# Opening of a fused two-block network reordered, and the idle products of TensorE taken out

## The chip, the cores and the metric

The kernel runs on one core of a Trainium2 chip. The metric is the device time of one execution in microseconds; smaller is better. The engines are named as in the profile: PE is TensorE (PEld its weight loads), DVE is VectorE, ACT is ScalarE, SP is SyncE, which issues all the DMAs here. hi and lo are the two parts into which an fp32 value is split for products in the fast format fp32r; a full product is hi x hi + lo x hi + hi x lo.

## The reference, cut

Two networks one after the other, on 256 tokens of width 1024, each two layers deep.

```python
# first block, layer l; x: tokens, xc: context tokens (256 each)
shift_x, scale_x, gate_x = split(silu(c) @ w_mod[l] + b_mod[l], 3)         # the same for c_ctx
hx = rmsnorm(x, norm_w[l]) * (1 + scale_x) + shift_x                        # the same for hc
px = hx @ w_in[l]          # retention, short conv, conformer conv, attention, gates
merged = sum(sigmoid(gate_i) * (branch_i @ w_branch[l, i]) for i in range(4))
x = x + gate_x * (merged @ w_out[l])
# second block, layer i; mod = silu(c_2) @ ada_w[i] + ada_b[i], six parts
h = rmsnorm(x, g0) * (1 + sc_m) + sh_m
y = rglru_mixer(h) if i == 0 else gla_mixer(h)
x = x + gt_m * rmsnorm(y, g1)
h = rmsnorm(x, g2) * (1 + sc_f) + sh_f
x = x + gt_f * rmsnorm(conv_ffn(h), g3)
```

## The kernel before, in words

Activations lie transposed: 8 tiles of 128 channels by 256 tokens (512 with the context, in layer 0 of the first block). Weights stream from HBM through a ring of three slabs of 1 MB (`stream`, SP's loop at line 1166). Each slab holds two weight tiles, the units; ACT writes the high part of a unit (line 1236), DVE the low part (line 1944), into four slots. `project` (line 610) makes one output tile: 8 products hi x hi, 8 with the low tokens, 8 with the low weights (lines 625, 627, 630). `project_group` (line 634) starts three tiles together and takes the token tiles in turn as they become ready (lines 601 to 603). Each result goes to one of 8 PSUM banks in turn and is evacuated by ACT (line 1222) or DVE.

The order of work is written by hand on each engine, with counting semaphores between them; a wait holds all that stands behind it on its engine.

The opening: SP issues params, the first table columns, the rows of c and c_ctx (1 MB, already spread over all partitions), then pairs of modulation weights (`start_pair`: a scale block of 1 MB for DVE, a shift block of 1 MB for PE), x, ctx, and the first weight slabs. ACT makes silu of the rows (line 1332). DVE makes the scales: each block of 128 outputs is a multiply and reduce over 1024 against a row (line 1977). PE makes the shifts (`shift_rows`, line 660: silu(c) as stationary operand; `shift_cols`, line 668: turned into columns). ACT squares x (line 1279), PE sums the squares over channels (`sum_all`, line 676), ACT takes the root, DVE the reciprocal (line 1845). DVE then writes normed tiles (line 1855), ACT their high parts with the shift (line 1316), DVE the low parts (line 1864), and the first group of projections starts. Behind it DVE computes the decays (lines 2020 to 2048) and, between other work, reductions for the second block's modulation (line 1981), whose weights SP issues between slabs (`IN_MODS`). The 31-tap convolution (line 2226) is DVE's longest piece; the weighted keys (line 2250) that PE needs at line 786 stand behind it.

`keep_clock(n)` (line 570) writes n products of a table with itself into the next free bank. Nobody reads them. It stands ahead of places where PE would wait: in the first merge, ahead of the output projections of each layer, in the RG-LRU and GLA outputs, in the sums ahead of GLA, and three times in `ffn`. The call in the retention loop never runs, since step 1 has a projection there in both layers. In `ffn` and ahead of GLA the stop is: sums of y (line 1001), residual on DVE, squares on ACT (line 1625), `sum_pairs` on PE (line 684, 16 passes), root, reciprocal, normed pairs, then the next projections.

Of the kernel before, what the change touches and what calls it, by code (L numbers as in the profile page):

```python
# [25 lines left out]
P = 128  # L26
# [28 lines left out]
IN_STAGE, IN_MODS = "in", (4, 4, 4, 3, 3, 3, 3)  # L55
# [55 lines left out]
def program(nc, io, counts):  # L111

    ctx = ExitStack()
    with ctx:
# [29 lines left out]
        c_rows_landed, c2_landed, shapes_landed = sem("c_rows_landed"), sem("c2_landed"), sem("shapes_landed")  # L144
# [164 lines left out]
        lam8, lam8n = small[:, 240:248], small[:, 248:256]  # L309
        warm = sbuf("warm", 16)  # L310
# [238 lines left out]
        def _(pe):  # L549
# [153 lines left out]
            for l in range(2):  # L703
# [113 lines left out]
                for n, (hd, g) in enumerate(units):  # L817
                    ret_scores(hd, g)
                    if n in in_ret:
                        project(in_ret[n], nx)  # L820
                    elif n == 1:
                        keep_clock(8)
                    if n:
                        ret_out(*units[n - 1])
# [95 lines left out]
                keep_clock(3 if l == 0 else 5)  # L920
# [44 lines left out]
            def ffn(l):  # L965
                keep_clock(9)
# [4 lines left out]
                keep_clock(3 if l else 7)  # L971
# [5 lines left out]
                keep_clock(7)  # L977
# [65 lines left out]
            keep_clock(4)  # L1043
# [4 lines left out]
            keep_clock(9)  # L1048
            sum_pairs("n2 1")
            keep_clock(7)  # L1050
# [72 lines left out]
            keep_clock(7)  # L1123
# [5 lines left out]
        def _(sp):  # L1129
            sp.dma_start(params[:], io["params"]).then_inc(params_landed, 16)  # L1130
            sp.dma_start(tables[:, 0:EARLY], io["tables"][:, 0:EARLY]).then_inc(early_landed, 16)
            sp.dma_start(shapes, io["c_rows"][:, 0:2 * D]).then_inc(c_rows_landed, 16)

            def start_pair(i):

                w = io["w_mod_t"][0][D + 256 * i:D + 256 * i + 256, :].rearrange("(j p) k -> p j k", p=P)
                sp.dma_start(start_blocks(START + i), w).then_inc(start_landed[START + i], 16)
                sp.dma_start(start_slot(i), by_rows(io["w_mod"][0])[:, :, 256 * i:256 * i + 256])\
                    .then_inc(start_landed[i], 16)
# [22 lines left out]
            start_pair(0)  # L1162
            sp.dma_start(xT[:, :, 0:S], by_rows(io["x"])).then_inc(x_landed, 16)
            sp.dma_start(xT[:, :, S:2 * S], by_rows(io["ctx"])).then_inc(x_landed, 16)
            start_pair(1)
            for n, (name, src, _) in enumerate(stream):
                if name == "w rgo 0":

                    sp.wait_ge(*vector.did(f"expo 1.{HEADS - 1}"))
                    sp.wait_ge(*scalar.did(f"q_dec 1.{HEADS - 1}"))  # L1170
                    sp.dma_start(level, io["level"]).then_inc(late_landed, 16)
                    sp.dma_start(gla_a, io["gla_w_alpha_2"][0]).then_inc(late_landed, 16)
                if n == 2:
# [25 lines left out]
                if RING + 1 <= n <= RING + len(IN_MODS):  # L1199
                    due.append((n, IN_STAGE, n - RING - 1, None))  # L1200
# [13 lines left out]
        def _(act):  # L1214
# [105 lines left out]
            def start_shift(k):  # L1320

                if k in (4, 6):
# [5 lines left out]
            def silu_rows(n):  # L1328

                act.wait_ge(c_rows_landed, 16 * n)  # L1330
# [6 lines left out]
            silu_rows(1)  # L1337

            for l in range(2):
                nx = 2 * S if l == 0 else S  # L1340
                groups = (0, 1) if l == 0 else (0,)
                if l == 0:
# [11 lines left out]
                act.wait_ge(shapes_landed, 16 * (l + 1))  # L1354
                if l == 0:

                    act.wait_ge(tables_landed, 16)
                    act.wait_ge(c2_landed, 16)
                    nc.scalar.activation(c2_row, c2_row, ACT.Silu).then_inc(*scalar.does("c2 row"))
                    at = PARAM_AT["decay"][0]  # L1360
                    nc.scalar.activation(lp[0], params[:, at:at + 24], ACT.Abs).then_inc(*scalar.does("lp abs"))
                    act.wait_ge(*scalar.did("lp abs"))
                    nc.scalar.activation(lp[1], lp[0], ACT.Exp, scale=-1.0).then_inc(*scalar.does("lp exp"))
# [462 lines left out]
        def _(dve):  # L1826
# [162 lines left out]

            def start_blocks_done(i):  # L1990

                dve.wait_ge(start_landed[i], 16)
                for j in range(2):
                    modulate_block("mod", 0, 2 * i + j, start_blocks(i)[:, j, :], start_scratch)
                vector.now[f"start mod {i}"] = vector.n
# [56 lines left out]
            for l in range(2):  # L2052
# [4 lines left out]
                if l == 0:  # L2057
                    dve.wait_ge(early_landed, 16)
                    dve.wait_ge(*scalar.did("c rows 1"))
# [6 lines left out]
                    for k in (0, 2, 4, 6):  # L2066
                        if k > 2:
                            start_blocks_done(START + k // 2)
                            low(k - 2)
                            low(k - 1)  # L2070
# [4 lines left out]
                        if k == 2:  # L2075
                            split_to(3)
                            low(0)
                            low(1)
# [4 lines left out]
                dve.wait_ge(shapes_landed, 16 * (l + 1))  # L2083
                dve.wait_ge(tables_landed, 16)
# [61 lines left out]
                if l == 0:  # L2146
                    settled()
                    for n in range(BT):
                        short_in(n, False)
                        if n == 0:  # L2150
                            decays()
                            dve.wait_ge(*scalar.did("c2 row"))
                        else:
                            mod_blocks(mod_plan[IN_STAGE, n - 1])
                    for k in range(SC_K):
# [740 lines left out]
```

## Time and profile before

| | us |
|---|---|
| runs, lowest / median / highest of 3 | 1831.96 / 1834.66 / 1835.02 |
| profiled execution | 1834.24 |
| its span, first to last instruction | 1832.5 |
| PE busy | 1765.7 (96%) |
| PE weight loads busy | 1564.7 (85%) |
| DVE busy | 1438.4 (78%) |
| ACT busy | 894.4 (49%) |
| mean granted clock of PE, of full | 0.994 |

The ends of matmuls are modelled, so a busy PE is not PE at its peak. An fp32 product runs as two passes, each an instruction of its own. On the timeline the bracket gives the idle time of the engine before the instruction and what ended it.

### The profile page before, as it was taken

How to read it: one execution, taken by the hardware profiler on the slowest of the kernel's cores; microseconds unless marked ns; L12 is line 12 of the kernel's file. 1: busy time of each engine (PE TensorE's matmuls, PEld its weight loads, DVE VectorE, ACT ScalarE, POOL GpSimd, SP SyncE). 2: the span in 40 equal slices, each digit the busy share in tenths (PEclk: the TensorE clock that was granted, in tenths of full speed). 3: DMA queues.
4: the chain of work that ended last, by engine and by line, in shares of the span. 5: the costliest groups of instructions: out<-in, count | busy, mean ns of one | idle time of the engine just before them, and what ended most of it. 6: DMA issues, size and time to landing. Idle time of an engine off the chain costs nothing.

```text
span 1832.5 us, 29617 instructions
## 1 busy us (share of the span) xinstructions
PE 1765.7 (96%) x11364; PEld 1564.7 (85%) x11364; DVE 1438.4 (78%) x2491; ACT 894.4 (49%) x1528; POOL 0.2 (0%) x4
## 2 busy tenths in 40 slices
PE   4999999999999999999999999999999989999998
PEld 1788887777888887988978999988999979989998
DVE  5789995558899898797866799878887478869864
ACT  3322334456232334443355755676656466567553
POOL 0000000000000000000000000000000000000000
PEclk8999999999999999999999999999999999999999
DMA  9564321212777776553421599552555625226543
GB/s 346 199 237 145 115 70 44 73 37 74 257 242 244 262 254 227 167 155 106 136 93 58 176 330 310 162 174 92 185 186 171 196 69 162 92 93 207 185 157 120
DMA packets 242332, 302.77 MB, mean 165 GB/s; under 512 B 6016, under 2 KB 223360, under 8 KB 241680
## 3 DMA queue, kind: packets, MB, share of 16 engines
q1 hardware_dynamic: 242192, 300.87, 49.9%
q8 instruction: 92, 1.51, 0.4%
q14 instruction: 48, 0.39, 0.1%
HBM read 299.79 MB, written 1.05 MB: 164 GB/s over the span
## 4 chain that ended last, share of the span: by engine, by line
PE 43%; DVE 8%; ACT 4%; issue 3%; DMA 0%; DVEq 0%; ACTq 0%
PE bank L625 10%; PE bank L627 10%; PE bank L630 10%; PE bank L601 2%; PE bank L603 2%; PE bank L602 2%; ACT w_hi L1236 1%; DVE w_lo L1944 1%; PE bank L956 1%; PE bank L957 1%; PE bank L958 1%; DVE stats L1845 1%; PE bank L684 1%; PE bank L1032 0%; DVE arena L2645 0%
## 5 line engine op out<-in xcount | busy, mean ns | idle before, releaser
L1944 DVE TENSOR_TENSOR w_lo<-ring,w_hi 128x1024 fp32r<-128x1024 f32 (+2 forms) x444 | 500.3, 1135 | 199.9 <-ACT w_hi L1236 197.3
L1236 ACT ACTIVATE w_hi<-ring 128x1024 fp32r<-128x1024 f32 (+2 forms) x444 | 434.2, 985 | 170.9 <-PE bank L630 95.9
L625 PE MATMUL bank<-h_hi,w_hi 128*128 128x256 f32 (+2 forms) x2366 | 418.2, 319 | 0.4
L630 PE MATMUL bank<-h_hi,w_lo 128*128 128x256 f32 (+2 forms) x2366 | 410.4, 315 | 0.0
L627 PE MATMUL bank<-h_lo,w_hi 128*128 128x256 f32 (+2 forms) x2366 | 410.4, 315 | 0.0
L625 PEld LDWEIGHTS bank<-h_hi,w_hi 128*128 128x128 f32 x2366 | 344.9, 188 | 35.5 <-issue 2.6
L627 PEld LDWEIGHTS bank<-h_lo,w_hi 128*128 128x128 f32 x2366 | 346.0, 188 | 29.9
L630 PEld LDWEIGHTS bank<-h_hi,w_lo 128*128 128x128 f32 x2366 | 346.1, 188 | 29.8
L1222 ACT ACTIVATE work<-bank 128x512 f32<-128x512 f32 (+1 forms) x138 | 68.3, 509 | 262.0 <-PE bank L630 194.5
L1222 ACT ACTIVATE arena<-bank 128x256 f32<-128x256 f32 (+4 forms) x125 | 56.5, 453 | 218.2 <-PE bank L630 148.3
L2226 DVE SCALAR_TENSOR_TENSOR arena<-arena,params 128x512 f32<-128x512 f32 (+1 forms) x240 | 131.1, 631 | 0.0
L1981 DVE CUSTOM_DVE_ANT_0 arena<-arena,c_row,params 128x1024 f32<-128x1024 f32 x96 | 120.1, 1281 | 11.6 <-DMA arena<-in_ada_w_t 11.5
L601 PE MATMUL bank<-h_hi,w_hi 128*128 128x256 f32 (+2 forms) x306 | 94.1, 308 | 18.2 <-DVE h_lo L1864 9.1
L1222 ACT ACTIVATE work<-bank,params 128x256 f32<-128x256 f32 x88 | 49.6, 564 | 90.4 <-DVE w_lo L1944 57.0
L602 PE MATMUL bank<-h_lo,w_hi 128*128 128x256 f32 (+2 forms) x306 | 91.8, 300 | 0.0
L603 PE MATMUL bank<-h_hi,w_lo 128*128 128x256 f32 (+2 forms) x306 | 91.7, 300 | 0.0
L601 PEld LDWEIGHTS bank<-h_hi,w_hi 128*128 128x128 f32 x306 | 59.3, 194 | 24.4 <-issue 12.5
L1977 DVE CUSTOM_DVE_ANT_0 arena<-arena,tables,params 128x1024 f32<-128x1024 f32 x48 | 60.7, 1282 | 18.8 <-DMA arena<-in_w_mod_t 18.8
L2588 DVE SCALAR_TENSOR_TENSOR work<-bank,params,work 128x255 f32<-128x255 f32 x88 | 42.4, 482 | 32.3 <-ACT work L1222 32.2
L625 PE MATMUL bank<-arena_r,w_hi 128*128 128x512 f32 (+2 forms) x306 | 64.8, 338 | 1.9 <-ACT w_hi L1236 1.7
L627 PE MATMUL bank<-arena_r,w_hi 128*128 128x512 f32 (+2 forms) x306 | 64.6, 337 | 0.0
L630 PE MATMUL bank<-arena_r,w_lo 128*128 128x512 f32 (+2 forms) x306 | 64.5, 337 | 0.0
(296 smaller groups left out, 2227.6 us busy)
## 6 DMA issues: line engine op xcount, KB each, us to landing
ring<-in_w_in SPq DMA_DIRECT2D x86, 1024.0 KB, 5.7
arena<-in_ada_w_t SPq DMA_DIRECT2D x96, 512.0 KB, 6.1
ring<-in_ffn_w_up SPq DMA_DIRECT2D x44, 1024.0 KB, 5.1
ring<-in_w_branch SPq DMA_DIRECT2D x32, 512.0 KB, 4.9
arena<-in_w_mod_t SPq DMA_DIRECT2D x32, 512.0 KB, 5.4
ring<-in_ffn_w_down SPq DMA_DIRECT2D x16, 1024.0 KB, 5.1
ring<-in_gla_w_in SPq DMA_DIRECT2D x12, 1024.0 KB, 5.4
ring<-in_w_out SPq DMA_DIRECT2D x8, 1024.0 KB, 6.3
```

The source lines that it names most:

```text
L601: pe.matmul(out, ws[0][:, k, :], hi, start=start, stop=False)
L602: pe.matmul(out, ws[0][:, k, :], lo, start=False, stop=False)
L603: return pe.matmul(out, ws[1][:, k, :], hi, start=False, stop=stop)
L625: pe.matmul(out[:, 0:n], w[0][:, k, :], hi(k, n), start=k == 0, stop=False)
L627: pe.matmul(out[:, 0:n], w[0][:, k, :], lo(k, n), start=False, stop=False)
L630: m = pe.matmul(out[:, 0:n], w[1][:, k, :], hi(k, n), start=False, stop=k == tiles - 1)
L1222: return nc.scalar.activation(dst, src, func, **kw)\
L1236: nc.scalar.activation(w_hi[u % PARTS][:, 0:src.shape[1], :], src, ACT.Copy)\
L1944: step(nc.vector.tensor_tensor(w_lo[u % PARTS][:, 0:nk, :], src, w_hi[u % PARTS][:, 0:nk, :].bitcast(F32), ALU.subtract), f"lo {u}", *(["u ...
L1977: step(nc.vector.tensor_tensor_reduce(w if v else scratch, w, c_rows[:, v, :], 1.0, param("b_mod", 2)[:, l, c:c + 1], ALU.mult, ALU.add, m ...
L1981: step(nc.vector.tensor_tensor_reduce(w, w, c2_row, 1.0, param("ada_b", 2)[:, l, c:c + 1], ALU.mult, ALU.add, mod2[l][:, c:c + 1]), name)
L2226: step(nc.vector.scalar_tensor_tensor(dst, src, cw[:, l, k, n:n + 1], dst, ALU.mult, ALU.add), name)
```

## The change

- c rows: the two loads of rows (c and c_ctx, c_2) go. DVE makes six tiles `c_diag` (each four 128x128 pieces: the identity times a column of silu(c)), PE multiplies them by ones (6 products of 128x512), ACT copies the results into `c_rows` and `c2_row`.
- Order of loads: both first scale blocks, x, ctx, the first shift block, slab 0, the second shift block, slab 1, then the other four blocks, slab 2, tables. `IN_AT` issues later reductions' weights up to one slab earlier.
- PE: the sums of squares first, then shift rows 0 and 1. ACT and DVE: weight splits in smaller steps between the normed tiles; the decays move to the time in which DVE waits for the rows.
- All calls of `keep_clock` go, and the function.

```diff
-IN_STAGE, IN_MODS = "in", (4, 4, 4, 3, 3, 3, 3)
+IN_STAGE, IN_MODS, IN_AT = "in", (4, 4, 4, 3, 3, 3, 3), (4, 5, 6, 7, 7, 8, 9)
+        c_diag = [t[:] for t in dve_t] + [stat, stat2]
-            def keep_clock(n):
-                b = state_["bank"]
-                if b >= BANKS:
-                    pe.wait_ge(*emptied(order[b - BANKS]))
-                for _ in range(n):
-                    pe.matmul(psum[b % BANKS][:, 0:S], ones, tables[:, 0:S], start=True, stop=True)
 # PE, opening
                     pe.wait_ge(early_landed, 16)
+                    for i in range(6):
+                        out = open_bank(f"c row {i}")
+                        pe.wait_ge(*vector.did(f"c diag {i}"))
+                        pe.matmul(out[:], ones_pp, c_diag[i], start=True, stop=True)\
+                            .then_inc(*tensor.does(f"filled c row {i}"))
+                    sum_all("n1 0", 2 * S, KT)
                     shift_rows(0)
-                    sum_all("n1 0", 2 * S, KT)
                     shift_cols(0)
 # PE, the idle products (places: 8 in the retention loop, never run; then as they run)
-                        if l == 0 and b == MERGE_ORDER[0] and i == 0:
-                            keep_clock(6)
-                keep_clock(3 if l == 0 else 5)        # ahead of out {l}
-                keep_clock(9)                         # ffn: ahead of the sums
-                keep_clock(3 if l else 7)             # ffn: ahead of the projections
-                keep_clock(7)                         # ffn: ahead of the down projection
-            keep_clock(4)                             # ahead of the RG-LRU output
-            keep_clock(9)                             # n2 1: ahead of the sums
-            keep_clock(7)                             # n2 1: behind the sums
-            keep_clock(7)                             # ahead of the GLA output
 # SP
-            sp.dma_start(shapes, io["c_rows"][:, 0:2 * D]).then_inc(c_rows_landed, 16)
-            start_pair(0)
+            start_scales(0)
+            start_scales(1)
             sp.dma_start(xT[:, :, 0:S], by_rows(io["x"])).then_inc(x_landed, 16)
             sp.dma_start(xT[:, :, S:2 * S], by_rows(io["ctx"])).then_inc(x_landed, 16)
-            start_pair(1)
+            start_shifts(0)
+                if n == 1:
+                    start_shifts(1)
                 if n == 2:
-                    start_pair(2)
-                    start_pair(3)
+                    for i in (2, 3):
+                        start_scales(i)
+                        start_shifts(i)
+                if n == 3:
                     sp.dma_start(tables[:, EARLY:shapes_at], ...).then_inc(tables_landed, 16)
-                    sp.dma_start(c2_row, io["c_rows"][:, 2 * D:3 * D]).then_inc(c2_landed, 16)
+                due += [(n, IN_STAGE, i, None) for i, at in enumerate(IN_AT) if at == n]
 # ACT
-            silu_rows(1)
+            (abs and exp of the decays, moved here)
+            for i in range(6):
+                row = c2_row if i >= 4 else c_rows[:, i // 2, :]
+                evacuate(f"c row {i}", row[:, 512 * (i % 2):512 * (i % 2) + 512], ...)
-                    square_all("n1 0", 2 * S, KT, lambda k: xT[:, k, :], also=lambda k: k == 3 and shift_row(0))
+                    square_all("n1 0", 2 * S, KT, lambda k: xT[:, k, :])
                     deviation("n1 0", 2 * S, D)
+                    split_to(1)
+                    shift_row(0)
                     shift_col(0)
+                    split_to(2)
                     shift_row(1)
-                    split_to(1)
                     shift_col(1)
-                    split_to(3)
                     modulated("n1 0", ..., start_shift, both_hi)      # start_shift(3) now does split_to(3)
 # DVE
+                    for i in range(6):
+                        for j in range(4):
+                            ins = nc.vector.tensor_scalar(c_diag[i][:, P * j:P * j + P], ident,
+                                                          csil[:, 4 * (i % 2) + j, i // 2:i // 2 + 1], None, ALU.mult)
+                    decays()
                     dve.wait_ge(*scalar.did("c rows 1"))
                     start_blocks_done(START)
                     start_blocks_done(START + 1)
                     inverse("n1 0", 2 * S)
-                    for k in (0, 2, 4, 6): ...
+                    modulation1(0, 0, 4); split_to(1); tile(0); tile(1); split_to(2); low(0); low(1)
+                    tile(2); tile(3); split_to(3); low(2); low(3)
+                    start_blocks_done(START + 2); ...; tile(4); tile(5)
+                    start_block_done(START + 3, 0); low(4); low(5); start_block_done(START + 3, 1)
+                    ...; tile(6); tile(7); low(6); low(7)
```

## Rows read from the trace of the kernel before

**Rows 1.** The page, part 2: TensorE's granted clock in tenths, 40 slices of 45.8 us.
```profile
PEclk8999999999999999999999999999999999999999
```

**Rows 2.** The instructions of line 576: duration in ns, first and last start.
```profile
L576 PE MATMUL bank<-tables x166: 377/379/382, 446.3 to 1763.0; 128*128 128x256 f32 x166
```

**Rows 3.** Stretches: length, PE PEld DVE ACT POOL busy, PEclk, DMA share, GB/s.
```profile
40.00:45.00 5.00, 2.63 (x6) 2.15 (x7) 5.00 (x9) 0.44 (x2) 0.00 (x0) 0.50 1.08 367
...
811.40:814.70 3.30, 3.30 (x9) 2.59 (x8) 3.30 (x7) 0.00 (x0) 0.00 (x0) 0.50 0.13 42
...
1596.00:1600.00 4.00, 4.00 (x24) 4.00 (x23) 1.85 (x6) 0.97 (x2) 0.00 (x0) 0.57 0.94 313
```

**Rows 4.** Timeline of the opening: start, length in us, instruction, idle before.
```profile
9.47 2.00 ACT L1332 ACTIVATE tables<-tables 128x1024 f32<-128x1024 f32 x2 [5.01 <-DMA tables<-in_c_rows]
...
12.25 1.28 DVE L1977 CUSTOM_DVE_ANT_0 arena<-arena,tables,params 128x1024 f32<-128x1024 f32 x1 [12.25 <-DMA arena<-in_w_mod_t]
...
21.19 2.19 ACT L1279 ACTIVATE work<-xT 128x512 f32<-128x512 f32 x4 [9.71 <-DMA xT<-in_ctx]
...
21.87 7.13 PE L676 MATMUL bank<-work,tables 128*128 128x512 f32 x16 [0.96 <-ACT work L1279]
...
29.86 3.35 DVE L1845 RECIPROCAL stats<-stats 128x512 f32<-128x512 f32 x1 [1.25 <-ACT stats L1222]
...
42.37 0.77 PE L601 MATMUL bank<-h_hi,w_hi 128*128 128x512 f32 x1 [8.87 <-DVE h_lo L1864]
...
48.72 3.62 PE L660 MATMUL bank<-arena,small 128*2 128x256 f32 x16
...
64.57 1.68 DVE L1864 SCALAR_TENSOR_TENSOR h_lo<-work,mods,h_hi 128x256 fp32r<-128x256 f32 x4 [4.84 <-ACT h_hi L1316]
...
69.80 1.98 PE L625 MATMUL bank<-h_hi,w_hi 128*128 128x512 f32 x8
```

**Rows 5.** Timeline, behind the opening: DVE at 142 us, PE at 256 us.
```profile
141.88 1.28 DVE L1981 CUSTOM_DVE_ANT_0 arena<-arena,c_row,params 128x1024 f32<-128x1024 f32 x1 [3.83 <-DMA arena<-in_ada_w_t]
...
255.89 3.90 PE L786 MATMUL bank<-arena 128*128 128x128 f32 x32 [1.03 <-DVE arena L2250]
```

**Rows 6.** Timeline of PE: the norm stop of ffn 0; the sums ahead of GLA.
```profile
1262.14 4.05 PE L576 MATMUL bank<-tables 128*128 128x256 f32 x18
...
1268.31 5.38 PE L684 MATMUL bank<-work,tables 128*128 128x256 f32 x16 [2.12 <-ACT work L1625]
...
1273.52 3.19 PE L576 MATMUL bank<-tables 128*128 128x256 f32 x14
...
1278.11 0.36 PE L601 MATMUL bank<-h_hi,w_hi 128*128 128x256 f32 x1 [1.41 <-DVE h_lo L1911]
...
1475.41 4.31 PE L684 MATMUL bank<-work,tables 128*128 128x256 f32 x16 [1.25 <-ACT work L1625]
```

**Rows 7.** Timeline of PE, ACT and DVE at idle products followed by ready work.
```profile
448.28 2.00 ACT L1332 ACTIVATE tables<-tables 128x1024 f32<-128x1024 f32 x2
...
1139.59 2.32 PE L576 MATMUL bank<-tables 128*128 128x256 f32 x10
...
1144.95 0.35 PE L601 MATMUL bank<-h_hi,w_hi 128*128 128x256 f32 x1 [1.26 <-ACT h_hi L1556]
...
1403.09 3.18 PE L576 MATMUL bank<-tables 128*128 128x256 f32 x14
...
1411.33 2.96 DVE L1944 TENSOR_TENSOR w_lo<-ring,w_hi 128x1024 fp32r<-128x1024 f32 x3 [0.16 <-ACT w_hi L1236]
...
1760.23 3.18 PE L576 MATMUL bank<-tables 128*128 128x256 f32 x14
...
1770.05 0.36 PE L956 MATMUL bank<-w_hi,h_hi 128*128 128x256 f32 x1 [0.96 <-ACT w_hi L1236]
```

**Rows 8.** Who PE waited for: us in total, times, longest.
```profile
PE bank L601 <- ACT arena L1222: 2.0, 1, 2.0
...
PE bank L625 <- ACT w_hi L1236: 1.7, 1, 1.7
```

More of the change, by code:

```diff
@@ L143, in program @@
         start_landed = [sem(f"start_landed{i}") for i in range(2 * START)]
[L144 removed]
+        c_rows_landed, shapes_landed = sem("c_rows_landed"), sem("shapes_landed")
         x_landed, late_landed, out_landed = sem("x_landed"), sem("late_landed"), sem("out_landed")
@@ L1320, in start_shift @@
             def start_shift(k):
+                if k == 3:
+                    split_to(3)
                 if k in (4, 6):
@@ L1328, in silu_rows @@
             def silu_rows(n):
-                act.wait_ge(c_rows_landed, 16 * n)
+                act.wait_ge(c_rows_landed, 16 * (n - 1))
                 for v in range(2):
@@ L1336, in _ @@
             nc.scalar.activation(small[:, 32:56], param("c_vec"), ACT.Silu).then_inc(*scalar.does("csil"))
-            silu_rows(1)
+            at = PARAM_AT["decay"][0]
+            nc.scalar.activation(lp[0], params[:, at:at + 24], ACT.Abs).then_inc(*scalar.does("lp abs"))
+            act.wait_ge(*scalar.did("lp abs"))
+            nc.scalar.activation(lp[1], lp[0], ACT.Exp, scale=-1.0).then_inc(*scalar.does("lp exp"))
+            for i in range(6):
+                row = c2_row if i >= 4 else c_rows[:, i // 2, :]
+                evacuate(f"c row {i}", row[:, 512 * (i % 2):512 * (i % 2) + 512],
+                         also=["c rows 1"] if i == 3 else ["c2 row"] if i == 5 else [])
             for l in range(2):
@@ L1345, in _ @@
                     act.wait_ge(x_landed, 32)
-                    square_all("n1 0", 2 * S, KT, lambda k: xT[:, k, :], also=lambda k: k == 3 and shift_row(0))
+                    square_all("n1 0", 2 * S, KT, lambda k: xT[:, k, :])
                     deviation("n1 0", 2 * S, D)
+                    split_to(1)
+                    shift_row(0)
                     shift_col(0)
+                    split_to(2)
                     shift_row(1)
-                    split_to(1)
                     shift_col(1)
-                    split_to(3)
                     modulated("n1 0", (0, 1), lambda k, g: mod1[0][:, k, g:g + 1], start_shift, both_hi)
[L1354 to L1363, printed above, removed]
+                if l:
+                    act.wait_ge(shapes_landed, 32)
                 def first_out(kind, n, late):
@@ L1988, in mod_blocks, with start_block_done @@
                     modulate_block(*m, mod_slot(m), stats)
+            def start_block_done(i, j):
+                if j == 0:
+                    dve.wait_ge(start_landed[i], 16)
+                modulate_block("mod", 0, 2 * i + j, start_blocks(i)[:, j, :], start_scratch)
+                if j:
+                    vector.now[f"start mod {i}"] = vector.n
             def start_blocks_done(i):
[L1992 to L1995, printed above, removed]
+                start_block_done(i, 0)
+                start_block_done(i, 1)
             def modulation1(l, a, b):
@@ L2058, in _ @@
                     dve.wait_ge(early_landed, 16)
+                    dve.wait_ge(*scalar.did("csil"))
+                    for i in range(6):
+                        for j in range(4):
+                            ins = nc.vector.tensor_scalar(c_diag[i][:, P * j:P * j + P], ident,
+                                                          csil[:, 4 * (i % 2) + j, i // 2:i // 2 + 1], None, ALU.mult)
+                            step(ins, *([f"c diag {i}"] if j == 3 else []))
+                    decays()
                     dve.wait_ge(*scalar.did("c rows 1"))
@@ L2065, in _ @@
                                       both_hi, both_lo)
[L2066 to L2070, printed above, removed]
+                    after(f"start mod {START + 1}")
+                    modulation1(0, 0, 4)
+                    split_to(1)
+                    tile(0)
+                    tile(1)
+                    split_to(2)
+                    low(0)
+                    low(1)
+                    tile(2)
+                    tile(3)
+                    split_to(3)
+                    low(2)
+                    low(3)
+                    for k in (4, 6):
+                        if k == 4:
+                            start_blocks_done(START + 2)
+                        else:
+                            start_block_done(START + 3, 0)
+                            low(4)
+                            low(5)
+                            start_block_done(START + 3, 1)
                         after(f"start mod {START + k // 2}")
@@ L2074, in _ @@
                         tile(k + 1)
[L2075 to L2078, printed above, removed]
                     low(KT - 2)
@@ L2082, in _ @@
                 step(nc.vector.memset(cx[l][:, :, 0:ng, S + 1:S + 2], 0.0), f"cx z1 {l}")
-                dve.wait_ge(shapes_landed, 16 * (l + 1))
-                dve.wait_ge(tables_landed, 16)
+                if l:
+                    dve.wait_ge(shapes_landed, 32)
                 def grouped(ap):
@@ L2147, in _ @@
                     settled()
+                    dve.wait_ge(*scalar.did("c2 row"))
                     for n in range(BT):
                         short_in(n, False)
[L2150 to L2153, printed above, removed]
+                        if n:
                             mod_blocks(mod_plan[IN_STAGE, n - 1])
+                    dve.wait_ge(shapes_landed, 16)
+                    dve.wait_ge(tables_landed, 16)
                     for k in range(SC_K):
```

7 lines of the change are left out of this document (2 added, 5 removed).

## Prediction, made before the changed kernel ran

> **What bounds the kernel now.** I read the slices of the page first: after the opening, TensorE (PE) is busy in nearly every slice and its granted clock is full nearly everywhere [rows 1]. So the end is set by PE's own products, and a change pays only where it removes idle time of PE, products of PE, or time at half clock. Next the group of line 576: 166 instructions, 83 fp32 products of two passes each, which compute nothing [rows 2]. They stand at thirteen places. A pass starts every 0.216 us (18 of them last 4.05 us, the last one 0.38), so they hold PE for 36 us. What matters is not that sum but, place by place, whether PE would have waited anyway.
>
> Then the clock. Beyond the opening it falls three times, each time for some 3.4 us: a stretch at 0.50 after the wait at 809 to 811 us, one inside the sums at 1268, one after 1595 [rows 3]. What came before each: a PE wait of 2.0 us, of 2.1 us, and one much like them before 1595; the next shorter wait, 1.7 us, was followed by no fall [rows 6, 8]. I take from this that a wait of about 2 us can bring the fall and one below 1.7 us doesn't. The price: PE at 0.50 delivers half, so 3.3 us of pure products lose 1.65 us. In the sums of line 684, which wait for ScalarE (ACT) as well, it is less: 5.38 us with a fall against 4.31 us without, 1.07 us [rows 6].
>
> Last the opening, read engine by engine on the timeline [rows 4].
>
> **Part 1, the front.** Before: the rows of c land at 9.4 us, the first scale block at 12.1, x and ctx at 21.2, the sums run 21.87 to 29.0, the reciprocal ends at 33.2, the first projection starts at 42.37 at half clock, the grouped start ends at 69.80 [rows 3, 4].
> The change removes the load of the rows (1 MB) ahead of everything, and moves one shift load (1 MB) behind ctx. One such load took 2.6 us (9.45 to 12.1) and ctx lands after five of them, so x and ctx land near 18.1: 3.1 us earlier. Instead of the load, VectorE (DVE) makes 24 diagonal pieces of 128x128 and PE 6 products of 128x512, ACT 6 evacuations. None of these shapes stands in the opening. For PE the bounds are 0.43 us a pass (the sums at full clock, 7.13 us for 16) and twice that cold: 12 passes, 5.2 to 10.3 us from about 5.4 us on, so done between 10.6 and 15.7; I take 13. ACT and DVE work beside it. The two scale blocks (8 reductions of at most 1.28 us) then take DVE from about 14 to 24, still ahead of the reciprocal. So this stretch is hidden in the wait for x. If the products took 10 us more, DVE would become late at the reciprocal; that is the cover.
> The new risk: PE stands from 13 to 18.7, so the sums start at half clock. At full clock they take 7.1 us, wholly cold 13.7; part cold I take 1.6 us more. Sums end near 27.5 instead of 29.0, the reciprocal near 31.7 instead of 33.2.
> From there the order is new: DVE splits two weight tiles (about 1.15 us each, as in [rows 7]) ahead of the first normed tiles and one ahead of the first low part, where it split four; but both shift rows (3.6 us of PE each) now stand behind the sums, 27.5 to 36, and ACT's first high part behind them, near 37.6. The first low part ends at 38.4: the first projection starts 3.9 us earlier, and warm. After it DVE is the chain: two tiles' low parts, a split, low parts, four reductions (4.9 us), two tiles, two reductions, low parts, two reductions, tiles, low parts. Adding up, low part 6 is there at 60.8 and 7 at 61.7, against 65.4 for tile 6 before, and the group ends near 65.0: **4.8 us earlier**. Bounds: PE alone (8 tiles of 9 products at 0.23 us, two shift rows) could end at 62.4, -7.4; with sums wholly cold and one more fall, 67, -3.
> Behind the front, the chain of some thirty short DVE instructions for the decays leaves the stretch of the first projections, and the ada loads are issued earlier in the stream. Before, DVE waited 3.8 us for such a load at 141.88, went into the 31-tap convolution late, and made PE wait 1.03 us at 255.89 [rows 5]. With DVE's work gone and loads earlier this wait goes: **-1.0** (bounds 0 and -1.03). Front: **-5.8**, between -3 and -8.4.
>
> **Part 2, no idle products, work that PE did too early or too late.** At three places the next real product was ready behind the last idle one, so removal can move it. At 1403.09 (14 passes, 2.84 us) the down projection of block 0 can start at once; the fourth weight tile's low part, which DVE finishes at 1412.4 whatever PE does, then ends a wait of about 0.7 us: **-2.1** (bounds 0 and -2.84) [rows 7]. At 446.28 (12 passes, 2.4 us) the second branch tile's weights are split only behind ACT's 2.0 us of silu at 448.28, which gives most of it back: **-0.7** (bounds 0 and -2.4). At 1760.23 (14 passes) the same start gains nothing: PE waits at 1770.05 for a weight part that stands behind DVE's low parts, and the wait grows from 0.96 to 3.8 us [rows 7]. At 700.85 (6 passes, 1.1 us) and 1139.59 (10 passes) too the projection begins earlier and stops at the last merged tile, at the same time as before; the wait at 1144.95 grows from 1.26 to 3.2 us [rows 7].
>
> **Part 3, the clock.** The waits of PE that remain, products and wait together: 6.1, 4.5, 5.2, 4.5, 5.2, 2.8 us around the three norm stops of the FFNs and GLA (for instance 1262.14 to 1268.31 and 1273.52 to 1278.11) [rows 6], 5.0 us ahead of the GLA output, 3.8, 3.2, 2.8 and 1.9 us at the others. By the 2 us reading nearly all of them bring a fall; three falls are there before. Terms, each a price of a fall times how much of the stretch is real work of PE:
> - 1144.95: 1.65 x 0.75 = 1.2; 700.85 (1.9 us, at the border): 0.4; the output of RG-LRU at 1234 (2.8 us), where DVE's scan paces PE: 0.3.
> - norm stop of ffn 0: the sums already fell (1.07 in hand), now they start cold, and the projections behind 1278.11 start cold too: 1.7.
> - norm stop ahead of GLA: sums 1.0, less what the four spaced GLA products hide: 0.6.
> - norm stop of ffn 1: sums 1.0, projections 1.5: 2.5.
> - down projection of ffn 1: 1.5.
> - the falls at 811 and 1596 of this profile stay likely, not certain: -1.0.
> Sum **+7.2**; bounds 0 (no more falls than now) and twice the sums and starts, some +14.
> The Trainium skill, "TensorE: Matmul & The Clock Gate", section "Why this matters for your kernels", speaks against this change: long idle gaps between bursts put the clock back to half. By that sentence alone the longer waits all pay, as in my terms; the row at 811 shows that a wait of 2.0 us was enough here.
>
> **The sum** goes against the profiled execution: 1834.24 us, of which 1832.5 are span and 1.7 lie around it; it is 0.4 below the median of the runs (1834.66). 1834.2 - 5.8 - 2.1 - 0.7 + 7.2 = 1832.8; I forecast **1833.0**.
>
> **The rivals.**
> 1. The forecast, the two halves cancel: 1830.5 to 1836. For it: each term has a row. Chance 0.50.
> 2. Slower: the clock stays low through a whole norm stop. Mechanism: a wait of 4.5 to 6 us on either side of 16 sum passes, so the sums run cold from end to end (16 x 0.43 = 6.9 instead of 4.3 us, three times: +4.7 beyond the terms) and the two groups of projections behind them start with a second cold stretch (+1.6 each): 1833 + 8 = 1841. It decides if the sums, cold from their first pass, don't bring the clock back; against it, at 1268 the sums themselves brought it back before their end. Chance 0.14.
> 3. Faster: most waits of 2.6 to 3.8 us bring no fall, or one that other waits cover. Terms fall from 7.2 to about 3: 1829. For it, three falls are a small sample. Chance 0.15.
> 4. Faster, the front gives more: PE-bound from the first product, -7.4 and -1.0: 1830.4. Chance 0.11.
> 5. The front does less than it says: PE cold in the sums and the shift rows behind them, so that the first projection starts at 41: only -2: 1836.8. Chance 0.10.
>
> **The numbers.** Range 1828.5 to 1839.5: it takes in cases 1, 3, 4, 5 and part of case 2. 0.2% (3.7 us) is about what a measurement of this kernel can tell from no change, so faster means under 1831.0 and slower over 1838.3. Faster 0.27 (cases 3 and 4 and a little of 1), slower 0.16 (2 and a little of 5), same 0.57.
>
> **What would show it.** Right: no product of line 576; x squares at 18 us; sums ending 27 to 28; first projection 38 to 39; steady projections from about 65; no wait ahead of line 786; the down projection of ffn 0 straight behind its last projection; clock at 0.50 in eight to twelve stretches, and the sums of line 684 above 5 us in all three stops. Wrong: sums of line 684 at 4.3 us after waits of 5 us (case 3), or near 7 us (case 2); a grouped start ending after 67 (case 5).

## The result, and the profile after

| | before | after |
|---|---|---|
| median (lowest to highest), us | 1833.93 (1830.94 to 1835.02) | 1840.6 (1837.78 to 1842.96) |
| ratio of after to before, 95% | | 1.0036 [1.0027, 1.0045] |
| profiled execution / its span | 1834.24 / 1832.5 | 1842.96 / 1841.1 |
| PE busy / mean granted clock | 1765.7 / 0.994 | 1754.8 / 0.979 |

The change made the kernel 6.7 us slower, where I had forecast 1.7 us faster; the time lies above my range. The profiled execution of after is the slowest of its eight, 2.4 us above the median, that of before 0.3 above; so the traces show a loss of 8.6 us in the span, and I book that one and come back to the difference.

The page, part 2, granted clock in 40 slices, now with three eights behind 1240 us, where [rows 1] has only nines:

```profile
PEclk8999999999999999999999999998999989989999
```

Stretches of after, PE alone: length, PE busy and instructions, PEclk, DMA share, GB/s. They answer to [rows 3].

```profile
702.90:706.20 3.30, 3.30 (x9) 0.50 0.73 245
808.70:812.00 3.30, 3.30 (x9) 0.50 0.21 71
1143.20:1146.50 3.30, 3.30 (x18) 0.50 0.03 10
1266.10:1272.80 6.70, 5.56 (x13) 0.50 0.00 1
1276.30:1283.00 6.70, 4.87 (x23) 0.50 0.01 2
1474.30:1481.00 6.70, 5.20 (x12) 0.50 0.00 0
...
1597.20:1603.90 6.70, 4.42 (x21) 0.50 0.95 313
1627.90:1634.60 6.70, 3.79 (x9) 0.50 0.00 0
```

Behind the opening, and up to the last microseconds of the span, the clock is at half in 13 stretches (not shown: 6.8 us at 1484, 3.4 us at 1235, 1495, 1642 and 1778), six of them 6.8 us long, 65 us in all; before there were three, 10 us in all. Such a double stretch occurs nowhere behind the opening of before.

The timeline of PE in after, opening and waits (idle before in brackets; where a line has x4, the view's window ended inside the row of products):

```profile
18.88 9.45 PE L669 MATMUL bank<-work,tables 128*128 128x512 f32 x16 [5.62 <-ACT work L1270]
39.21 0.47 PE L594 MATMUL bank<-h_hi,w_hi 128*128 128x512 f32 x1 [2.30 <-DVE h_lo L1857]
66.16 1.98 PE L618 MATMUL bank<-h_hi,w_hi 128*128 128x512 f32 x8
252.25 3.90 PE L784 MATMUL bank<-arena 128*128 128x128 f32 x32 [1.03 <-DVE arena L2268]
447.25 1.21 PE L618 MATMUL bank<-arena_r,w_hi 128*128 128x512 f32 x4 [1.64 <-ACT w_hi L1227]
702.30 0.47 PE L594 MATMUL bank<-arena_r,w_hi 128*128 128x512 f32 x1 [1.97 <-ACT h_hi L1549]
1142.38 0.36 PE L594 MATMUL bank<-h_hi,w_hi 128*128 128x256 f32 x1 [3.18 <-ACT h_hi L1549]
1267.24 6.47 PE L677 MATMUL bank<-work,tables 128*128 128x256 f32 x16 [5.87 <-ACT work L1618]
1278.13 0.55 PE L594 MATMUL bank<-h_hi,w_hi 128*128 128x256 f32 x1 [4.42 <-DVE h_lo L1904]
1414.98 0.36 PE L594 MATMUL bank<-h_hi,w_hi 128*128 128x256 f32 x1 [0.93 <-DVE w_lo L1937]
1475.80 6.29 PE L677 MATMUL bank<-work,tables 128*128 128x256 f32 x16 [5.13 <-ACT work L1618]
1486.46 1.86 PE L1042 MATMUL bank<-work,params 128*16 128x256 f32 x4 [4.36 <-ACT work L1629]
1599.48 0.55 PE L594 MATMUL bank<-h_hi,w_hi 128*128 128x256 f32 x1 [4.90 <-DVE h_lo L1945]
1630.82 5.60 PE L677 MATMUL bank<-work,tables 128*128 128x256 f32 x16 [5.11 <-ACT work L1618]
1640.84 0.36 PE L594 MATMUL bank<-h_hi,w_hi 128*128 128x256 f32 x1 [2.68 <-DVE h_lo L1904]
1777.16 0.36 PE L949 MATMUL bank<-w_hi,h_hi 128*128 128x256 f32 x1 [3.99 <-ACT w_hi L1227]
```

The same instructions of before that the rows ahead of the prediction don't show:

```profile
706.45 0.47 PE L601 MATMUL bank<-arena_r,w_hi 128*128 128x512 f32 x1 [0.65 <-ACT h_hi L1556]
1484.09 1.02 PE L1055 MATMUL bank<-work,params 128*16 128x256 f32 x4 [1.34 <-ACT work L1636]
1595.65 0.36 PE L601 MATMUL bank<-h_hi,w_hi 128*128 128x256 f32 x1 [1.88 <-DVE h_lo L1952]
1626.51 4.31 PE L684 MATMUL bank<-work,tables 128*128 128x256 f32 x16 [1.22 <-ACT work L1625]
1635.24 0.36 PE L601 MATMUL bank<-h_hi,w_hi 128*128 128x256 f32 x1 [1.38 <-DVE h_lo L1911]
```

How to read them together: take the start of one instruction in both traces; the difference is what has been won or lost up to there, and the step from one difference to the next belongs to what lies between. 66.16 against 69.80 in [rows 4] is -3.64, 252.25 against 255.89 is again -3.64, 702.30 against 706.45 is -4.15, and so on to 1777.16 against 1770.05, +7.11, and +8.6 at the end. The steps, beside the terms of the prediction:

| stretch | predicted | in the traces |
|---|---|---|
| front, to the end of the first group | -4.8 | -3.64 |
| wait at 252 | -1.0 | 0 |
| first merge | -0.7 | -0.51 |
| fall at 702, output of layer 0 | +0.4 | +1.59 |
| falls at 811 and 1596 of before, priced as likely but not certain | -1.0 | 0 at the first (808 in after), and +0.48 at the second (1597 in after), now double |
| 1142, output of layer 1 | +1.2 | +1.51 |
| output of RG-LRU, 1235 | +0.3 | 0 |
| norm stop of ffn 0, its sums and its group | +1.7 | +1.09 and +2.26 |
| down projection of ffn 0 | -2.1 | -1.91 |
| norm stop ahead of GLA, sums and what follows | +0.6 | +1.98 and +1.48 |
| norm stop of ffn 1, sums and group | +2.5 | +1.29 and +1.51 |
| down projection of ffn 1 | +1.5 | +1.5 |
| sum | -1.4 | +8.6 |

### The profile page after: what moved, and what is told of

It reads as the page before. It is cut to its first block, busy times and chain, and to the rows that moved or that the text cites. A ratio compares the mean times of both kernels' runs of the same rounds, so it can differ in the third digit from the quotient of the medians.

```text
span 1841.1 us, 29336 instructions
## 1 busy us (share of the span) xinstructions
PE 1754.8 (95%) x11210; PEld 1552.5 (84%) x11210; DVE 1444.2 (78%) x2514; ACT 894.6 (49%) x1530; POOL 0.2 (0%) x4
## 4 chain that ended last, share of the span: by engine, by line
PE 32%; DVE 16%; ACT 6%; issue 4%; DMA 1%; DVEq 0%; ACTq 0%
PE bank L618 6%; PE bank L620 6%; PE bank L623 6%; DVE w_lo L1937 5%; PE bank L594 2%; PE bank L595 2%; PE bank L596 2%; ACT w_hi L1227 2%; DVE work L2612 2%; DVE work L2606 2%; ACT work L1213 1%; PE bank L949 1%; PE bank L950 1%; PE bank L951 1%; PE bank L677 1%
## 5 line engine op out<-in xcount | busy, mean ns | idle before, releaser
L618 PEld LDWEIGHTS bank<-h_hi,w_hi 128*128 128x128 f32 x2366 | 345.6, 189 | 35.4 <-issue 2.7
L623 PEld LDWEIGHTS bank<-h_hi,w_lo 128*128 128x128 f32 x2366 | 346.0, 188 | 29.7
L594 PEld LDWEIGHTS bank<-h_hi,w_hi 128*128 128x128 f32 x306 | 62.9, 205 | 29.2 <-ACT h_hi L1624 7.7
L596 PEld LDWEIGHTS bank<-h_hi,w_lo 128*128 128x128 f32 x306 | 63.1, 206 | 1.9
```

Of the source, the lines that this page charges most:

```text
L594: pe.matmul(out, ws[0][:, k, :], hi, start=start, stop=False)
L596: return pe.matmul(out, ws[1][:, k, :], hi, start=False, stop=stop)
L618: pe.matmul(out[:, 0:n], w[0][:, k, :], hi(k, n), start=k == 0, stop=False)
L623: m = pe.matmul(out[:, 0:n], w[1][:, k, :], hi(k, n), start=False, stop=k == tiles - 1)
```

## The experiments

The front alone is the changed kernel with the idle products back; further kernels start from it or from the changed kernel. Medians are in us, ratios to the kernel before on the same chip: 1833.6 beside e1 to e4, 1833.7 beside e5 to e8, 1835.2 beside e9.

| kernel | median (lowest to highest) | ratio, 95% |
|---|---|---|
| e1, idle products out, old front | 1842.01 (1841.53 to 1843.75) | 1.0044 [1.0029, 1.0059] |
| e2, front alone | 1830.69 (1828.84 to 1831.68) | 0.9980 [0.9970, 0.9989] |
| e3, e2 less two idle places | 1828.92 (1827.39 to 1831.14) | 0.9973 [0.9963, 0.9984] |
| e4, e2 with a new pace of the convolution | 1827.91 (1826.70 to 1830.78) | 0.9969 [0.9959, 0.9980] |
| e5, waits cut to about 3 us | 1837.42 (1832.52 to 1842.18) | 1.0016 [1.0004, 1.0028] |
| e6, e2 with idle products in the opening | 1828.16 (1825.22 to 1830.62) | 0.9964 [0.9953, 0.9976] |
| e7, all gains | 1822.59 (1821.67 to 1825.32) | 0.9938 [0.9923, 0.9953] |
| e8, idle products ahead of the sums only | 1832.94 (1831.62 to 1837.49) | 0.9998 [0.9989, 1.0008] |
| e9, e7 with the last two falls covered | 1821.86 (1820.20 to 1823.74) | 0.9933 [0.9919, 0.9947] |

### The two halves apart: e1 and e2

```diff
 # e1: the kernel before
-            def keep_clock(n): ...
-                keep_clock(...)          # at all places
 # e2: the changed kernel
+            def keep_clock(n): ...
+                keep_clock(...)          # at all places of before
```

> The kernel before, with every idle product taken out and its old front kept. Theory A (the two halves add up, and the loss is the clock): the change lost 8.6 us in the span of its profile and its front gave 3.6, so this half alone costs 12.3 us: 1846, ratio 1.0067. The granted clock falls at the same places as in the changed kernel, twice as long (6.8 us) in the norm stops. Theory B (part of the loss comes from the new front, whose earlier loads and shifted times collide with what follows): the loss here is 8 us or less, 1842 at most. Theory C (my prediction's own terms: 7.2 us of clock less 2.8 of earlier work): 1838.

> The changed kernel with all idle products put back where they were. Theory A: the front alone gives the 3.6 us that stand at 252 us of the changed trace and keeps them to the end: 1830.3, ratio 0.9980; the clock falls beyond the opening three times for 3.4 us, as in the kernel before. Theory B: the front brings losses of its own behind 260 us, 1832 to 1834. Prediction's term of 5.8: 1828.2.

Measured: +8.4 and -2.9, together +5.5 against +6.7 (5.0 to 8.3 by its interval) for the change. So within the noise the halves add up, and the loss is that of the idle products; the front brings none. Theory B falls by e2, whose time it put at 1832 to 1834; e1 alone would not decide, since 1842.01 lies on theory B's bound. Of theory A, e2 gave the time (1830.7 for 1830.3, with four falls where three were expected), and e1 did not: 8.4 us for 12.3, having been worked out from one trace. e1's own span is 9.5 us above that of before, yet its profiled execution was its slowest. In it, two waits that were followed by a fall in after were followed by none (stretches of e1, PE alone):

```profile
705.00:709.00 4.00, 3.93 (x17) 1.00 0.69 237
809.70:813.70 4.00, 3.96 (x17) 1.00 0.15 50
1140.70:1147.30 6.60, 5.08 (x24) 0.50 0.22 73
```

The first two are the stretches behind waits of 1.97 and 1.96 us, the same to 0.01 us as in after, where the clock fell behind both. At 811 of before it fell behind the same wait [rows 3]. A wait of 2 us is one that may bring a fall or not. The third line is a double fall behind a wait of 2.88 us, at the place where after has a single one behind 3.18 us: the length of the wait alone doesn't decide how long the clock stays down, either.

### Two places where work was ready: e3

```diff
-                            keep_clock(6)                    # first merge
-                keep_clock(7)                                # ahead of down, ffn 0 only
```

> As the front alone, with idle products put back everywhere except at the two places where real work was ready behind them: the 12 passes in the first merge and the 14 passes ahead of the down projection of ffn 0. Theory A: the first gives 0.5 and the second 1.9 us (shifts at these places in the changed kernel), and the waits left there, 1.6 and 0.9 us, bring no fall of the clock: 1827.9, 2.4 below the front alone, ratio to before 0.9967. Rival: the gains exist only because PE had lost time before these places, so DVE and ACT were ahead of it; with PE in time the waits grow and give most back: less than 1 us below the front alone.

The median is 1828.9 where theory A had 1827.9. In the trace both gains came: against e2 the steps are 0.54 and 1.87 us, and the new wait for the fourth low part is there (timeline of PE in e3):

```profile
1409.85 0.36 PE L602 MATMUL bank<-h_hi,w_hi 128*128 128x256 f32 x1 [0.94 <-DVE w_lo L1955]
```

Then the clock fell at 1481 and 1488 (0.50 in both stretches), among waits of 1.34 and 0.6 us that are those of e2 to the hundredth, and took 1.6 us back in that execution. By the medians e3 is 1.8 below e2, with intervals that overlap. By the two steps of the trace the rival falls: the gains don't depend on lost time before them.

### Why the wait at 252 stayed: e4

The timeline of DVE in after, ahead of the wait:

```profile
137.88 1.92 DVE L2240 TENSOR_SCALAR arena<-arena,params 128x512 f32<-128x512 f32 x4
...
211.27 1.23 DVE L1937 TENSOR_TENSOR w_lo<-ring,w_hi 128x1024 fp32r<-128x1024 f32 x1 [0.71 <-ACT w_hi L1227]
...
244.33 1.22 DVE L1937 TENSOR_TENSOR w_lo<-ring,w_hi 128x1024 fp32r<-128x1024 f32 x1 [0.68 <-ACT w_hi L1227]
245.47 3.39 DVE L2244 SCALAR_TENSOR_TENSOR arena<-arena,params 128x512 f32<-128x512 f32 x5
248.90 1.29 DVE L2255 TENSOR_TENSOR arena<-bank,arena 128x512 f32<-128x512 f32 x2
250.22 2.48 DVE L2268 TENSOR_TENSOR arena<-bank,small 128x512 f32<-128x512 f32 x4
```

DVE enters the convolution at 137.88, before at 147.58: 9.7 us earlier, while PE is 3.64 us earlier. The early start is what I had said. But DVE takes a weight split after every sixth tap, and a split waits for a unit that ACT converts at PE's pace. So DVE gives back what it has beyond PE's own lead, 0.2 to 0.7 us per unit at fourteen splits (the kernel before has one such wait, 0.66 us ahead of its last split), and reaches its last split when PE lets it; five taps, two products and the weighted keys stand behind it whatever the lead was.

```diff
-                        if (BT * k + n) % 6 == 5:
+                        i = BT * k + n
+                        if (i % 7 == 6) if i < 28 else ((i - 28) % 6 == 5):
```

> As the front alone, with one change in VectorE's order: in the 31-tap convolution of both layers the first four weight splits come after seven taps each instead of six, so that one tap instead of five stands behind the last split. Theory P (in the changed kernel VectorE entered the convolution 9.7 us earlier and gave it all back in waits for the weight units, one per six taps; what stands behind its last split, 5 taps, 2 products and the weighted keys, sets the 1.03 us wait of PE): the wait ahead of the states (line 784 of the changed kernel) goes, 1.0 us below the front alone. Rival Q (the wait is set by something else, the kT banks or ScalarE's evacuations of them): the wait stays at 1.03 and the time is that of the front alone. In layer 1 the same pace could make VectorE late by up to 2.6 us for PE's units; then the time is above the front alone.

Timeline of DVE in e4:

```profile
244.59 1.22 DVE L1955 TENSOR_TENSOR w_lo<-ring,w_hi 128x1024 fp32r<-128x1024 f32 x1 [0.68 <-ACT w_hi L1245]
245.74 0.75 DVE L2263 SCALAR_TENSOR_TENSOR arena<-arena,params 128x512 f32<-128x512 f32 x1
...
248.49 0.69 DVE L2274 TENSOR_TENSOR arena<-bank,arena 128x512 f32<-128x512 f32 x1 [1.29 <-PE bank L631]
```

One tap stands behind the last split, DVE now waits 1.29 us for PE instead of PE for DVE, and the wait of 1.03 is gone. Theory P holds; from the first projection to 295 us the trace is 1.4 us shorter than e2's. The median is 2.8 below e2's, with intervals that overlap; the part above 1.4 is not the pace's by any row (the clock fell twice behind the opening in this trace, four times in e2's; behind a wait of 2.34 us ahead of 806.87 it was 1.00 here).

### What makes a fall long: e5 and e8

```diff
 # both: the changed kernel, keep_clock(n) with n as follows, else none
 # e5: sums 6, 4, 4; behind the sums 3, 3, 0; GLA output 4; down of ffn 1: 2
 # e8: sums 9, 9, 9
```

> The changed kernel with idle products at seven places, in counts that leave every wait of TensorE at 2.7 to 3.4 us: ahead of the sums 6, 4 and 4, behind them 3, 3 and none, 4 ahead of the GLA output, 2 ahead of the down projection of ffn 1, none elsewhere. In the changed kernel waits of 2.0 to 4.0 us brought falls of 3.4 us, waits of 4.4 to 5.9 us falls of 6.8 us. Theory D (the length of the wait sets the length of the fall): no fall of 6.8 us is left in the norm stops, sums of line 677 near 5.4 us instead of 6.3 to 6.9; 3 to 4 us below the changed kernel: 1837. Rival E (any wait above some 2 us brings the whole loss, what follows sets how long the clock stays low): the falls of 6.8 us stay, 1840.

Stretches of e5, PE alone:

```profile
1267.20:1273.80 6.60, 5.98 (x14) 0.50 0.01 2
1475.40:1478.70 3.30, 3.30 (x9) 0.50 0.03 5
1478.90:1485.40 6.50, 3.36 (x15) 1.00 0.00 0
1598.30:1601.50 3.20, 3.20 (x17) 0.50 0.89 308
1601.70:1605.00 3.30, 3.30 (x30) 1.00 0.00 0
```

Its timeline:

```profile
1474.39 5.55 PE L685 MATMUL bank<-work,tables 128*128 128x256 f32 x16 [3.40 <-ACT work L1636]
```

With waits of 2.7 to 3.4 us, five of the six double stretches are gone: the sums at 1474 recover the clock half-way through (5.55 us instead of 6.29), and the projections at 1598 after 3.4 us. The one at 1267 stayed (6.71 us of sums behind a wait of 3.13). The median is 3.2 below after's, as theory D said, with intervals that just touch and the widest scatter of all kernels here. So rival E falls, and shorter waits cost less in sum; but the length sets no fixed price. Against theory D stand two double falls, this one and the one behind 2.88 us in e1; and at 1278.95 a wait of 3.13 us was followed by no fall at all. What else decides stays open.

> The changed kernel with idle products only ahead of the three sums of the norm stops (9 each), none behind them and none elsewhere. Theory A (each place pays for itself): the losses at the sums go (1.1, 2.0 and 1.3 us in the changed trace), those of the groups behind them (2.3, 1.5, 1.5), of the down projection (1.5) and at 702 and 1142 (1.6, 1.5) stay: 1836.2. Rival H (a wait of 4.4 us behind warm sums costs more than behind cold ones, or less, since the whole stop counts as one): the group behind 1278 then loses 3.3 us, or under 1 us, instead of 2.3.

The profiled execution took 1837.49, the slowest of its ten and 1.3 above theory A's time; the median is 1832.94, 3.3 below it, so by the median theory A missed: three places of thirteen gave back 7.7 us by the medians, where its terms had 4.4. In the trace the three sums ran warm (4.31 us each). Behind them the waits of 4.42 and 4.91 us brought falls of 6.8 us as in after, but that of 4.36 us one of 3.4 us where after has 6.8 us behind the same wait, that of 2.68 us ahead of 1636.98 none, and the stretch from the group at 1278.88 to the wait in the down projection at 1415.86 took 136.98 us, in after 136.85, in e3 without a fall 134.62: 2.3 us in both, so rival H falls at that place. Eight of ten executions lie at or below 1833.3 and two above 1836.8; which falls those eight were spared, no trace shows, since only one execution has one.

### The opening: e6

```diff
+                    keep_clock(10)
                     sum_all("n1 0", 2 * S, KT)
                     shift_rows(0)
```

> As the front alone, and ten more idle products (20 passes, about 4.3 us at full clock) between the row products and the sums of squares in the opening, where TensorE waited 5.6 us for x. In the changed kernel the sums lasted 9.45 us, 2.3 more than the 7.13 at full clock, and the reciprocal followed them. Theory F (half clock in the sums is what the front gave less than I predicted): sums 7.1 us, the reciprocal 2.2 us earlier, 2 us below the front alone: 1828.7. Rival G (behind the reciprocal VectorE and the weight parts are the chain, so that the gain shrinks on the way to the end of the first group): less than 0.8 us below the front alone. The group ends at 66.2 in the changed kernel; theory F 64.1, rival G 65.5 or more.

Timeline of PE in e6:

```profile
13.31 4.48 PE L577 MATMUL bank<-tables 128*128 128x256 f32 x20
...
18.36 7.13 PE L677 MATMUL bank<-work,tables 128*128 128x512 f32 x16 [0.57 <-ACT work L1289]
...
249.39 3.90 PE L793 MATMUL bank<-arena 128*128 128x128 f32 x32 [1.03 <-DVE arena L2287]
```

The sums are back at 7.13 us, and PE is 3.1 us ahead of e2 at 249 us (0.6 of it because the sums could begin that much earlier in this execution). The grouped start ends at 63.30, in e2 at 66.24; rival G had 65.5 or more. By the medians it gives 2.5 us, on another chip and with intervals that overlap. Theory F holds: the half clock in the sums, 2.3 us, was what the new front had lost on the way.

### All together: e7 and e9

```diff
 # e7: e4 with
-                            keep_clock(6)          # first merge
+                keep_clock(4 if l == 0 else 6)     # ahead of out {l}
+                keep_clock(11 if l else 13)        # sums of ffn
+                keep_clock(5 if l else 9)          # behind them
+                keep_clock(8 if l else 0)          # down
+            keep_clock(5), (11), (9), (10)         # RG-LRU output; GLA: sums, behind, output
+                    keep_clock(10)                 # opening, as in e6
+                    keep_clock(3)                  # layer 1, ahead of ret_k
+            keep_clock(2)                          # ahead of rga
 # e9: e7 with
+                    keep_clock(4)                  # ahead of the first group
+                if k in (2, 4, 6): keep_clock(1)   # between the products of gla z
```

> All that gave something, together, and idle products sized to the whole wait: the new front with ten in its wait for x, seven taps to the first four splits of the convolution, none in the first merge and none ahead of the down projection of ffn 0, and at the other places so many that 0.2 to 0.9 us of each wait are left (4, 6, 5, 13, 9, 11, 9, 10, 11, 5, 8), with 3 more ahead of the keys of layer 1 and 2 ahead of the RG-LRU gates. From the kernel with the pace, 1827.9: merge -0.5, down -1.9, front -2, two falls of 3.4 us at 1262 and 1590 gone, -1.1 and -1: 1821.4. Theory A: no fall of the clock behind the opening. Rival: the gains of removed work come back as waits, and products sized to the wait overrun it in places: 1825 or more.

Stretches of e7, PE alone:

```profile
100.00:1480.00 1380.00, 1355.12 (x8385) 1.00 0.49 163
1484.40:1487.60 3.20, 3.20 (x17) 0.50 0.85 271
1490.00:1820.00 330.00, 324.60 (x2635) 1.00 0.43 142
```

Timeline of e7:

```profile
112.33 2.11 PE L631 MATMUL bank<-h_hi,w_lo 128*128 128x512 f32 x8 [1.33 <-DVE w_lo L1959]
...
1262.43 4.31 PE L685 MATMUL bank<-work,tables 128*128 128x256 f32 x16 [0.39 <-ACT work L1640]
```

1822.6, 11 us below the kernel before and 18 below the changed one, 1.2 above the time expected. The clock is full from 100 to 1480 us, the sums last 4.31. Against theory A one fall is left behind the opening, where waits of 0.5 and 0.6 us follow one another. A new wait of 1.33 us at 112 is one for VectorE: its weight split stands behind reductions, one of which waited 2.4 us for its weights at 99.

> The kernel with all gains together (1822.6) and four more idle products ahead of the first group of projections, where 2.3 us of wait are left in the opening and the clock falls once more at 37 us, and one in each of the three 0.6 us waits between the GLA products, where it falls once more at 1484 us. Theory A: neither fall is left; the one at 1484 costs 1.5 us there, the one at 37 about 1 us on TensorE, of which VectorE's chain gives back a part: 1.5 to 2.5 us less, 1820.5. Rival: what is left behind the opening is VectorE's chain (low parts, weight splits, reductions), and at 99 us it waited 2.4 us for a load of the second block's modulation, so that an earlier start only lengthens that wait: 1822.5, no change that can be measured.

One stretch of e9, PE alone:

```profile
28.00:1816.00 1788.00, 1757.84 (x11380) 1.00 0.49 163
```

Full clock from the sums of the opening to 2 us ahead of the end of the span, so neither fall is left. The median is 0.7 below e7's, in another series; the ratios 0.9933 and 0.9938 can't be told apart, so whether these two places gain anything is open. Both kernels beat both of the case.

## Why the prediction was wrong

By the table of steps, I was 10.0 us off in the profiled execution: 7.5 by the clock, 2.2 by the front, 0.4 by the earlier work. Against the median, 1840.6 for 1833.0, it is 7.6.

- The clock, the step that failed. I worked out 1.65 us for pure products at half clock, and that held: 1.59, 1.51 and 1.5 us at 702, 1142 and 1777, with one fall each ahead of dense products. What was mis-sized is how long the clock stays down. All three falls of before came behind waits of about 2 us, and I took their 3.4 us for the length of every fall. Behind the 4.4 to 5.9 us waits of after it was 6.8. The stops of ffn 0 and GLA were priced at 1.7 and 0.6 and cost 3.35 and 3.46; with the double fall at 1597 that is 5.0 of the 7.5. e5 shows five of these six places with a short fall or none once the waits are cut, and the sixth unchanged. Most of the rest are single falls that I had priced as chances, 0.4 at 702 and -1.0 for the two of before: all three came in the profiled execution, though e1 shows that behind the same waits two of them can stay out.
- Rival 2 had this mechanism (sums slow nearly from end to end, 6.47 and 6.29 us) in two of the three stops; in the third the sums took 5.60 us, the clock back before their end. Its 1841 is near the median in part by luck: its clock terms, 15.2 us, fit the trace's 14.7, but its front was 2.2 us too good, and the profiled execution took 1842.96. I gave it 0.14. The reason against it was one row: at 1268 the sums had brought the clock back before their end. That row stood behind a wait of 2.1 us, and I used it for waits more than twice as long. The clock's part in the trace, 14.7 us, lies just above my upper bound of +14, and the range didn't reach even to that bound.
- The Trainium skill, "TensorE: Matmul & The Clock Gate", section "Why this matters for your kernels", advises against idle gaps between bursts because the clock goes back to half. The trace of after agrees: behind each of its ten waits of 2.66 to 5.87 us the clock was at half. It fell behind 1.96 and 1.97 us as well, and in other kernels here not behind 2.68 and 3.13 us, so a gap of that length may or may not pay.
- The front. x squares at 18.19, first projection at 39.21 (38.5 predicted), as worked out. The group ended at 66.16 instead of 65.0: sums of 9.45 us where I had 7.13 and 1.6 more, so 0.7 longer, and one more fall at 41 us, which I had set only in the bound. The -1.0 at 252 was wrong in its reason: a lead of an engine that is fed at PE's pace doesn't reach the end of its chain. e4 turned it into a gain by changing what stands behind the last split.
- The earlier work was right: -0.51 and -1.91 for -0.7 and -2.1, with the new wait of 0.93 us where I had 0.7. The places that gain nothing gained nothing, and the waits at 1144.95 and 1770.05 in [rows 7] grew from 1.26 to 3.18 and from 0.96 to 3.99, as said.
- The signs "clock at 0.50 in eight to twelve stretches" and "sums above 5 us in all three stops" were near or met (13 stretches; 6.47, 6.29 and 5.60 us). The signs came as I had said; what they cost was priced too low.

## What to carry to other kernels

A product that computes nothing is worth what the clock would lose behind the wait that it fills; put it where PE waits anyway, size it to that wait, and leave it out where real work is ready. Price a fall of the clock from a row behind a wait of the same length, since a longer wait can cost twice as much, and give the price a spread, since the same wait can cost nothing. A lead won on a helper engine is worth something only if nothing between it and its consumer is fed at the consumer's pace.

## What the runs showed of the hardware

- Waits of the same length don't always bring the same: behind 1.96 to 1.97 us the clock fell in before and after and not in e1; behind 1.34 and 0.6 us it fell in e3 and not in e2; behind 1.2 to 1.3 and 0.8 us, near 1200, it fell in e2 and e3 and not in before and after. A wait of 3.13 us was followed by none in e5, one of 2.34 us by none in e4. The times of e5, with many waits near 3 us, scatter most from execution to execution (9.7 us between lowest and highest); after (5.2) and e6 (5.4), which has few long waits, don't differ, so no rule follows from it.
- Idle products need not cover a wait wholly: with 0.4 us left the sums ran at 4.31 us, with 1.25 us (before) and 1.78 us (e8) left too, with 2.1 us left at 5.38.
- What a double fall costs depends on how much of it passes in the wait itself. The one at 1276.3 had 1.8 us in the wait and 4.9 us of busy PE behind it and cost 2.26 us; the one at 1627.8 had 3.0 us in the wait and 3.8 us of busy PE and cost 1.29.
